# A hybrid decoder step: sample rows, row blocks and the first weight re-ordered in the opening

## What is computed

```
for i in range(2):
    h = rmsnorm(y, norm_w[i])            # y: x_prompt (512 x 1024) and x_sample (8 x 1024)
    if i == 0: out = ssd_mixer(h, ...)   # h @ w_in (1024 x 5152), conv, SSD recurrence, gate, norm, @ w_out
    else:      out = short_conv_mixer(h, ...)
    y = y + out
y = rmsnorm(y, final_norm_w)

def rmsnorm(x, w):
    return x * rsqrt(mean(x * x, axis=-1) + EPS) * w
```

## Time and profile before

| | |
|---|---|
| median of 3 runs | 926.73 us (925.05 to 927.12) |
| span of the profiled execution | 925.8 us |
| PE busy | 885.2 us, 96% |
| DVE, ACT, POOL busy | 627.2, 405.6, 142.9 us |
| mean granted clock of TensorE | 0.993 |

### The profile page before, as it was taken

How to read it: one execution, slowest core, us unless ns; L and a number is a source line. 1 busy time by engine, 2 the same in 40 slices (tenths; PEclk the granted TensorE clock), 3 DMA queues, 4 the chain that set the end, 5 groups by cost and what they waited for, 6 DMA issues and landing times.

```text
span 925.8 us, 19336 instructions
## 1 busy us (share of the span) xinstructions
PE 885.2 (96%) x7385; PEld 870.9 (94%) x7385; DVE 627.2 (68%) x1039; ACT 405.6 (44%) x757; POOL 142.9 (15%) x95
## 2 busy tenths in 40 slices
PE   5999899899989999979999999999999999999996
PEld 5899889899989998968999999999999999999996
DVE  4579999979997899987555555555555555564543
ACT  6556857545864576744432222222222222243343
POOL 5303531243143312450000000000000000000000
PEclk9989999999999999999999999999999999999999
DMA  7427636563475437723333333333333333222212
GB/s 170 115 69 208 181 86 196 167 156 104 138 210 158 133 105 218 199 74 92 92 91 114 91 91 91 91 91 91 91 91 91 91 91 91 91 88 94 92 45 93
DMA packets 162993, 108.00 MB, mean 117 GB/s; under 512 B 5000, under 2 KB 155152, under 8 KB 162368
## 3 DMA queue, kind: packets, MB, share of 16 engines
q1 hardware_dynamic: 123876, 76.15, 28.4%
q10 hardware_dynamic: 38756, 30.61, 11.5%
q0 software_dynamic: 304, 0.48, 0.3%
HBM read 95.35 MB, written 12.14 MB: 116 GB/s over the span
## 4 chain that ended last, share of the span: by engine, by line
PE 53%; DVE 2%; issue 1%; ACT 1%; POOLq 0%; POOL 0%; DVEq 0%; ACTq 0%
PE pair L1818 20%; PE bank L1818 19%; PE pair L2083 5%; PE bank L2083 5%; PE pair L1878 3%; DVE ybuf L1710 0%; PE bank L1891 0%; POOLq L90 0%; ACT sqb L818 0%; DVE acc L1680 0%; ACT xT L976 0%; DVE sqs L1398 0%; DVE ylo L1645 0%; PE bank L2148 0%; DVE yr L1370 0%
## 5 line engine op out<-in xcount | busy, mean ns | idle before, releaser
L527 ACT ACTIVATE whi<-raw 128x1024 fp32r<-128x1024 f32 x136 | 143.6, 1058 | 338.2 <-PE bank L1818 136.8
L1818 PE MATMUL pair<-hhi,whi 128*128 128x260 f32 x1136 | 232.4, 286 | 0.3 <-DVE acc L1195 0.3
L1818 PE MATMUL pair<-hhi,wlo 128*128 128x260 f32 x1136 | 229.6, 284 | 0.0
L1818 PE MATMUL pair<-hlo,whi 128*128 128x260 f32 x1136 | 229.1, 283 | 0.0
L1065 DVE TENSOR_TENSOR wlo<-raw,whi 128x1024 fp32r<-128x1024 f32 x132 | 184.2, 1396 | 22.7 <-ACT whi L527 20.6
L1818 PEld LDWEIGHTS pair<-hhi,whi 128*128 128x128 f32 x1136 | 176.0, 190 | 2.8 <-DVE acc L1195 1.7
L1818 PEld LDWEIGHTS pair<-hlo,whi 128*128 128x128 f32 x1136 | 175.9, 189 | 0.0
L1818 PEld LDWEIGHTS pair<-hhi,wlo 128*128 128x128 f32 x1136 | 175.9, 189 | 0.0
L1818 PE MATMUL bank<-hhi,whi 128*128 128x260 f32 x512 | 103.1, 282 | 0.9 <-ACT sqs L512 0.9
L1818 PE MATMUL bank<-hhi,wlo 128*128 128x260 f32 x512 | 103.2, 283 | 0.0
L1818 PE MATMUL bank<-hlo,whi 128*128 128x260 f32 x512 | 103.0, 283 | 0.0
(11 more groups left out here) (256 smaller groups left out, 1303.6 us busy)
## 6 DMA issues: line engine op xcount, KB each, us to landing
raw<-in_sc_w_in SPq DMA_DIRECT2D x64, 512.0 KB, 4.0
raw<-in_ssd_w_in SPq DMA_DIRECT2D x40, 512.0 KB, 4.0
abc<-a_rows ACTq DMA_DIRECT2D x16, 512.0 KB, 4.7
sample<-in_state_ssm ACTq DMA_DIRECT2D x16, 512.0 KB, 7.9
out_new_ssm_s<-sample ACTq DMA_DIRECT2D x16, 512.0 KB, 4.3
raw<-in_ssd_w_out SPq DMA_DIRECT2D x16, 512.0 KB, 3.9
raw<-in_sc_w_out SPq DMA_DIRECT2D x16, 512.0 KB, 3.5
sample<-bc_rows ACTq DMA_DIRECT2D x4, 1024.0 KB, 6.8
```

The source lines that it names most:

```text
L527: act.activation(whi[:, slot, :], raw[:, slot % RAW, :], ACT.Copy).then_inc(hi_done, 1)
L1818: mm = pe.matmul(b, w[:, slot, k * P:(k + 1) * P], h[:, k, cols], start=(k == 0 and i == 0), stop=(k == KT - 1 and i == 2))
```

## The change

It does six things in the opening; nothing behind it is touched.

1. POOL raises `lo_done` and `sqs_done` first of all, no longer behind its nine DMA issues, and waits for the first weight (`raw_in[0]`) before it issues them.
2. SP issues the load of the `dt` columns (`dwr`) behind the second weight instead of behind the first.
3. PE turns `rowsA` straight after the raw sample rows, then blocks 0 and 1, then the scaled sample rows, then blocks 2 and 3.
4. DVE copies `colA` ahead of block 0's scaling, reduces the sample squares after it, and scales the sample rows itself, after block 1.
5. ACT takes the sample root behind block 1's.
6. ACT copies the first weight ahead of every `hhi`.

```
@@ sync
-                if n == 1:
+                if n == 2:
                     sp.dma_start(dwr[:, :, :], w_in0[:, :, DI + XBC:DI + XBC + HEADS]).then_inc(dtw_in, 16)
@@ gpsimd
+            pool.sem_inc(lo_done, SLOT)
+            pool.sem_inc(sqs_done, 1)
             pool.memset(ident[:, :], 0.0).then_inc(consts, 1)
...
+            pool.wait_ge(raw_in[0], 16)
             pool.dma_start(rowsB[0:8, :], ins["norm_w"][1].rearrange("(t c) -> t c", c=P)).then_inc(par_in, 16)
...
-            pool.sem_inc(lo_done, SLOT)
-            pool.sem_inc(sqs_done, 1)
...
-            pool.wait_ge(xss_root, 1)
-            pool.tensor_scalar(xs_norm, x_nat[4], ssq[0:NB, 4:5], None, ALU.mult).then_inc(xsn_done, 1)
             low(0, 0, 16)
@@ scalar
             x_rstd(0)
-            x_rstd_sample()
             x_sum(1)
             x_rstd(1)
+            x_rstd_sample()
...
             x_rstd(3)
+            high(0, 0, 16)
             act.wait_ge(xsw_done, 1)
             act.activation(hhi[:, :, SEQ:T], xs_w.rearrange("p (k b) -> p k b", b=NB), ACT.Copy).then_inc(hs_hi, 1)
-            h_high(0)
-            h_high(1)
-            high(0, 0, 16)
-            for k in range(2, KT):
+            for k in range(KT):
                 h_high(k)
@@ vector
-            dve.wait_ge(xss_sq, 1)
-            dve.tensor_reduce(ssq[0:NB, 4:5], xs_norm, AX, ALU.add).then_inc(xss_sum, 1)
...
-            normalise(0, 1)
-            normalise(1, 1)
             dve.wait_ge(row_t, 1)
             dve.tensor_scalar(colA[:, 0:n0], bank[6][:, 384:384 + n0], 0.5, None, ALU.mult)
             dve.tensor_copy(colA[:, n0:P], bank[6][:, 384 + n0:512]).then_inc(row_c, 1)
+            normalise(0, 1)
+            dve.wait_ge(xss_sq, 1)
+            dve.tensor_reduce(ssq[0:NB, 4:5], xs_norm, AX, ALU.add).then_inc(xss_sum, 1)
+            normalise(1, 1)
+            dve.wait_ge(xss_root, 1)
+            dve.tensor_scalar(xs_norm, x_nat[4], ssq[0:NB, 4:5], None, ALU.mult).then_inc(xsn_done, 1)
+            normalise(2, 1)
             dve.wait_ge(xst_done, 1)
...
-            normalise(2, 1)
             normalise(3, 2)
@@ tensor
-            pe.wait_ge(xn_done, 1)
-            for k in range(KT):
-                transpose(bank[k][:, 0:P], x_norm[0][:, k * P:(k + 1) * P])
+            pe.wait_ge(row_in, 48)
+            transpose(bank[6][:, 384:512], rowsA[:, :]).then_inc(row_t, 1)
+            for t in range(2):
+                pe.wait_ge(xn_done, t + 1)
+                for k in range(KT):
+                    if t == 0 and k == 6:
+                        pe.wait_ge(row_c, 1)
+                    transpose(bank[k][:, t * P:(t + 1) * P], x_norm[t][:, k * P:(k + 1) * P])
             pe.wait_ge(xsn_done, 1)
...
-            pe.wait_ge(row_in, 48)
-            transpose(bank[6][:, 384:512], rowsA[:, :]).then_inc(row_t, 1)
...
```

More of the change, by code:

```diff
@@ L379, in _, with low @@
             pool.memset(eps[:, 1:2], 4 * EPS).then_inc(consts, 1)
+            def low(n, slot, turn):
+                pool.wait_ge(hi_done, n + (1 + SLOT))
+                pool.wait_ge(raw_in[slot % RAW], turn)
+                pool.tensor_tensor(wlo[:, slot, :], raw[:, slot % RAW, :], whi[:, slot, :].bitcast(F32), ALU.subtract).then_inc(lo_done, 1)
+            pool.wait_ge(raw_in[0], 16)
             pool.dma_start(rowsB[0:8, :], ins["norm_w"][1].rearrange("(t c) -> t c", c=P)).then_inc(par_in, 16)
@@ L1065, in low @@
                 dve.tensor_tensor(wlo[:, slot, :], raw[:, slot % RAW, :], whi[:, slot, :].bitcast(F32), ALU.subtract).then_inc(lo_done, 1)
-            dve.wait_ge(x_in[4], 16)
-            dve.scalar_tensor_tensor(xs_norm, x_nat[4], 1.0 / D, x_nat[4], ALU.mult, ALU.mult).then_inc(xss_sq, 1)
-            dve.wait_ge(xss_sq, 1)
-            dve.tensor_reduce(ssq[0:NB, 4:5], xs_norm, AX, ALU.add).then_inc(xss_sum, 1)
             def normalise(t, parts):
@@ L1076, in normalise @@
                     dve.tensor_scalar(x_norm[t][:, cols], x_nat[t][:, cols], ssq[:, t:t + 1], None, ALU.mult).then_inc(xn_done, 1)
-            normalise(0, 1)
-            normalise(1, 1)
+            dve.wait_ge(x_in[4], 16)
+            dve.scalar_tensor_tensor(xs_norm, x_nat[4], 1.0 / D, x_nat[4], ALU.mult, ALU.mult).then_inc(xss_sq, 1)
             dve.wait_ge(row_t, 1)
@@ L1733, in _ @@
             mm.then_inc(xst_done, 1)
-            pe.wait_ge(row_in, 48)
-            transpose(bank[6][:, 384:512], rowsA[:, :]).then_inc(row_t, 1)
-            for t in range(1, 4):
-                for k in range(KT):
-                    if k == 0:
-                        pe.wait_ge(xn_done, t + 1)
-                    if t == 1 and k == 6:
-                        pe.wait_ge(row_c, 1)
-                    if t == 1 and k == 7:
-                        pe.wait_ge(xsw_done, 1)
-                    if t == 3 and k == KT // 2:
-                        pe.wait_ge(xn_done, 5)
-                    mm = transpose(bank[k][:, t * P:(t + 1) * P], x_norm[t][:, k * P:(k + 1) * P])
-                    if t == 3:
-                        mm.then_inc(xn_t, 1)
+            pe.wait_ge(xn_done, 3)
+            for k in range(KT):
+                if k == 7:
+                    pe.wait_ge(xsw_done, 1)
+                transpose(bank[k][:, 2 * P:3 * P], x_norm[2][:, k * P:(k + 1) * P])
+            for k in range(KT):
+                pe.wait_ge(xn_done, 4 + k // (KT // 2))
+                transpose(bank[k][:, 3 * P:4 * P], x_norm[3][:, k * P:(k + 1) * P]).then_inc(xn_t, 1)
             def project_dt():
```

## The result

The changed kernel takes **930.34 us**, the median of 12 runs (929.03 to 934.97), beside 927.25 for 12 runs of the kernel before on the same chip (924.61 to 929.98). The ratio is 1.0040, with a 95% interval of 1.0025 to 1.0055: slower. The forecast was no change, 926.4. Two further sets of the same changed kernel, taken with the experiments, gave 1.0023 and 1.0052; the means over all sets are 931.1 against 927.7.

What follows compares the result with a forecast made beforehand. PE, busy 96% of the span, was taken as the bound, the change's worth being decided before its unbroken stream. Terms -0.62 and +0.3 summed to -0.3 us: 926.4 beside the median, range 923.9 to 928.6.

Steps and rivals of the forecast that it cites:

- R: The moment PE can turn the weight rows rowsA, which now stands ahead of every row block; taken as 8.6 us.
- item 4: Landing of the weight rows, read from ACT's DMA queue: R = 8.6, bounds 6.2 and about 11.4, making item 3's term +0.3.
- item 2: Sample scaling moved from POOL (3.17) to DVE: 0.73 us, beside PE's second row block.
- item 3: Opening chain on PE, DVE and ACT: block 3 turned at R + 7.8, today 16.09; term R - 8.3, PE last.
- item 5: Weights: first lands 11.4 to 14.5, POOL's issues end 16.3 to 19.4, its difference 18.7 to 21.8; cost nothing.
- item 1: First weight copy ahead of all hhi on ACT: DVE's idle 0.62 goes, term -0.62.
- Rival D: Weight lands as late as today, 17.4, and its copy holds every hhi: +1.5, 928.2; chance 0.03.
- C: Rival: weight rows come late, R above 10.8; at 11.4 the sum is +2.5, 929.2; chance 0.06.
- near 18.8: Expected start of the first projection on PE, with no hole after it.
- The signs of being wrong: First projection before 17.5 or after 20.5 counts against item 3; PE waiting for POOL's difference counts against item 5.
- the prediction's first paragraph: PE is busy all of 20 to 40 us, so the change's worth is decided ahead of the first projection at 19.17.
- Rival B: PE falls to half rate in the opening, granted clock 0.50 before block 0's turning: +2.9, 929.6; chance 0.07.

Runs made afterwards that it cites:

- e1_hold: The changed kernel with POOL's first difference held until DVE's difference of the sample rows is done: 925.75 us, ratio 0.9981; second set 926.81, ratio 1.0002.
- e2_again: A second set of e2_rows_late, unaltered: 925.62 us, ratio 0.9990 to the kernel before.
- e2_rows_late: The changed kernel with the weight rows turned behind block 1 and colA copied behind block 2's scaling: 924.65 us, ratio 0.9967 to the kernel before.
- e5: The kernel before with sample scaling on DVE and rows turned behind block 1; POOL's issues, SP's order and ACT's weight copy unaltered: 926.07 us, ratio 0.9979.
- e3: The kernel before with only the weight's part (POOL's DMAs behind the first weight, dt columns later, weight copy first on ACT): 928.96 us, ratio 1.0015.
- d1: The kernel before with two idle ACT copies (1.3 us) ahead of the first hhi, lengthening PE's pause: 930.58 us, ratio 1.0026.
- e4: The kernel before with two-input POOL operations on unused data, released together with DVE's sample difference: 925.28 us in one execution.

## Why the prediction was wrong

**What held.** R was 8.93 (forecast 8.6, item 4). DVE scaled the sample rows in 0.81, in the second set 0.74 (0.73, item 2). Block 3 was turned at 16.90; R + 7.8 gives 16.73 (item 3), though at R = 8.6 the forecast stood at 16.4. The weight landed at 11.8 and was copied at 15.25 (11.4 to 14.5, and 15.3); POOL's issues ended at 17.0 and its difference at 19.39 (16.3 to 19.4, and 18.7 to 21.8; item 5). In e1_hold DVE ends its last `hlo` at 23.56; 23.49 in before, less the 0.62 of item 1, plus the 0.85 by which that run turned block 3 later, gives 23.72. So item 1's term is real, but it only pays for R. With the stall away, the second projection starts 0.08 and 0.40 later than before, where the sum had 0.3 earlier, and the two medians are 0.2% below before and level with it: the sum was right to within 0.7 us. Rival D was wrong, and so was C: R stayed far below 10.8. One consequence I got wrong in passing: the first projection "near 18.8" came at 20.02 even in e1_hold, with nothing lost, since what counts is DVE's last `hlo` and not when PE begins. The signs of being wrong pointed at the wrong item. A first projection after 20.5, and it came at 21.24, was to speak against item 3, whose chain held; item 5 was to be wrong if PE waited for POOL's difference, which it never did.

**What failed** is item 5's "Cost nothing". I placed POOL's first difference, which stood at 18.90, so that it would end between 18.7 and 21.8, and asked only whether PE would have to wait for its result. I never asked what it runs beside. DVE's sample difference (14.91) stood over 3 us from any POOL operation in before (one ends at 11.40, the next starts at 18.90); in the changed kernel both become free behind the same weight copy, within 0.6 us, and DVE's was held for 2.8 us. Its eight successors on DVE are the pace of the first projection, as the prediction's own first part says, so the loss went straight to the end: 1.22 from e1_hold to the changed kernel at the second projection. Why only 1.22 and not 2.8: DVE had 1.45 of idle time there, in which it waited for ACT's `hhi`.

The trace of before had the price. Further on DVE makes `wlo` itself for most weights, by the same operation as POOL's first:

```profile
L1065 DVE TENSOR_TENSOR wlo<-raw,whi x132: 1206/1225/3400, 52.1 to 892.5; 128x1024 fp32r<-128x1024 f32 x132
...
218.73 2.63 POOL L442 TENSOR_TENSOR sample<-sample 128x1024 f32<-128x1024 f32 x1 [3.64 <-DVE sample L1363]
219.04 3.40 DVE L1065 TENSOR_TENSOR wlo<-raw,whi 128x1024 fp32r<-128x1024 f32 x1
```

The three times are the shortest, the median and the longest in ns. The longest, 3.40, began 0.3 behind a POOL operation and ended 1.1 behind its end, about its own length alone: the same stall, in the trace that the prediction was made from.

**The second half of the loss** failed the prediction's first paragraph: what the change is worth was to be "decided ahead" of the first projection, because PE has no hole from 20 to 40. The profiled execution lost 1.30 there and 4.0 in all, and the rest goes with stretches at half rate. In the second set's profiled execution one lies right behind the first projection's start, and that one's second projection starts at 34.21:

```profile
14.00:22.00 8.00, 5.28 (x30) 0.99 0.54 83
```

(the clock begins to fall at 21.8, the end of this window; from 18 to 26 its mean is 0.79). In the other two it lies at 98, 166 and 265, behind pauses that leave before's clock alone.

How far the stall brings these stretches on is not settled. For it speaks that e1 differs from the changed kernel by one wait, and that on one chip the clocks are 0.9902 and 0.9855. Against a plain rule speak the fourteen profiled executions. Of the four with a pause of 1.17 to 1.30 ahead of the first projection none has half rate in it or right behind it; of the ten with 1.55 to 3.56 seven have, and the three without are e2_again (1.89) and the changed kernel itself, at 2.40 and 2.43. The second set of the changed kernel has before's mean clock. No run moved the stream and left the pause as it was.

**Rival B** had the mechanism of half rate, with 0.07, and a wrong reading of before. It says that TensorE turns block 0 "at full pace" today, 1.71 a block, and that the trace doesn't show half rate there. The trace does show it. Four turnings take 1.06 in the opening and 0.66 later in the same execution:

```profile
95.08 0.66 PE L1720 MATMUL bank<-ident,xs 128*128 128x128 f32 x4 [0.54 <-DVE xs L1217]
```

The granted clock reads 1.00 for the opening because the trace's record of it begins only at 17.9 in before and at 19.5 in the changed kernel; a stretch ahead of the record reads as 1.00. Where the record begins in the middle of the turnings, at 9.9 in e2_rows_late, four that start at 7.89 take 1.06 and four at 11.08 take 0.66. So in before and in the changed kernel all four blocks are turned at 1.2 GHz. B's price could not come on top of that, its test by the granted clock before 20 us could not have shown it, and a block priced at 1.71 in item 3 takes little more than half of that once the clock is up, as in e2 and e5. This changes nothing in the sum, since both kernels turn all blocks so.

**Also open:** why DVE's operation already stands before POOL's recorded start, 0.6 us in the changed kernel and 1.4 in e3. The queued POOL operation must be part of it, since e1 held just that back. That it stands in the queue is not enough: in e2_rows_late the sample difference runs at 12.95, with the same operation queued behind seven DMA issues and 3.6 away, and takes 0.23. The part played by the issues wasn't tried apart.

**The version to keep** is e2_rows_late: 6.7 us below the changed kernel in the medians on one chip (925.62 and 932.31), and 0.3% below before in the first set, 0.1% in the second, which alone is not clear of no change. Over e1_hold it gains 1.1 and 1.2 in the medians, since nothing stands ahead of block 0; that is within the spread of either. That the rows' turning ahead of block 0 was the costly part of the change was in the prediction's item 3, as the reason why a saving of 2.4 on the sample scaling gave +0.3; I treated it as given and not as the thing to undo.

## What to carry to other kernels

When an operation of GpSimd is moved, look at what VectorE runs at its new place, and not only at who waits for its result: a 0.2 us difference on SBUF tiles became 3 us. Where both become free behind the same event, let the short one go first; here the wait that does so moved POOL's operation by 0.03 us. And price a stall ahead of TensorE's stream with the pause that it makes there, since behind a longer pause the clock may fall: in d1 0.50 of delay at DVE's last `hlo` became 2.16 at the second projection. And read the rate of TensorE's first instructions from their durations, beside the same instruction later on, before trusting a granted clock of 1.00.

## What the runs showed of the hardware

The first unexpected thing is the stall. Measured: the difference of 128x64 takes 0.21 to 0.23 with POOL idle or issuing a DMA (before, e1, e2), and 3.02, 3.25, 3.00 and 3.89 ahead of POOL's 128x1024 difference (the three sets of the changed kernel, e3); two 128x512 scalings take 0.87 alone and 2.48 beside two POOL additions of 1.13 and 1.11 (e4). POOL's own operation is not slowed, 2.37 beside 2.39. DVE operations with an input from PSUM are not touched: three `hlo` take 2.08 beside POOL's difference in e1, and in before two take 1.41 beside it at 19.43 and 1.41 at 17.33, with POOL idle:

```profile
17.33 1.41 DVE L1095 SCALAR_TENSOR_TENSOR hlo<-pair,colA,hhi 128x512 fp32r<-128x512 f32 x2 [2.21 <-ACT hhi L558]
```

The Trainium skill has this (SBUF — State Buffer, "Who interferes with whom"): VectorE with two SBUF inputs, or in one of its two-port modes, shares a pair of ports with GpSimd, and the pair is locked for a whole instruction. By that rule, which speaks against this change, item 5 would have held a term; with the numbers measured since, some 2.8 less 1.45, +1.4, and the forecast would have been 927.8, still short of 930.34. The traces agree with the lock where POOL's operation covers 128 partitions, e4 with the case of `tensor_scalar`. They don't agree where it is the scaling of 8 partitions: POOL had started first, at 8.23, and DVE's scaling at 9.77 took its usual 0.75. And the page says that whoever starts first has the pair, while here DVE's record began first (16.46 against 17.02, 14.88 against 16.32) and yet it was DVE that waited. On both points the measurement decides, with the reserve that the profile gives POOL's spans only roughly.

TensorE's clock is the other. All turnings of the opening run at 1.2 GHz, 1.06 for four, after a time in which PE had done nothing but the raw sample rows; full rate is there from 17.9 in before, with PE at work without a pause since 11.46. It then fell in or right behind pauses of 1.55 to 3.56 ahead of the dense stream in seven of ten profiled executions, and in two of the changed kernel's three also at pauses of 2.0 to 2.4 that leave before's clock at 1.00. One profile can't tell whether a kernel does this: the same program does it in one execution and not in the next.
